# Opening of a backbone step: ten repeated filter products, the root taken ahead of the sine, and the second angle moved between two multiplications of x

## What is computed

```python
def rmsnorm(x, g):
    xf = x.astype(jnp.float32)
    y = xf * lax.rsqrt(jnp.mean(xf * xf, axis=-1, keepdims=True) + EPS)
    return (y * g.astype(jnp.float32)).astype(x.dtype)
...
    h = jnp.sin(freq * (feats @ fw1.astype(f32) + fb1.astype(f32)))
    h = jnp.sin(freq * (h @ fw2.astype(f32) + fb2.astype(f32)))
    h = (h @ fw3.astype(f32)).reshape(L, 2, 2, D_HY)
...
    sh1, sc1, g1, sh2, sc2, g2 = jnp.split(mod[:, None, :].astype(dt), 6, axis=-1)
    h = rmsnorm(x, n1) * (1 + sc1) + sh1
    u = h @ w_in
```

## Time and profile before

| | us |
|---|---|
| median of 3 runs | 2548.91 |
| lowest and highest run | 2544.83, 2552.96 |
| the profiled execution's own time | 2545.34 |
| its span in the profile | 2543.6 |

### The profile page before, as it was taken

The page is one execution under the profiler, slowest core; times in us unless marked ns, Lnnn a source line. Parts: engine busy times, 40 slices in busy tenths (PEclk is TensorE's granted clock), DMA queues, the critical chain, the costliest instruction groups (busy, mean ns, idle before and its releaser), DMA issues. The chain is left out here.

```text
span 2543.6 us, 34536 instructions
## 1 busy us (share of the span) xinstructions
PE 2466.6 (97%) x13482; PEld 2094.6 (82%) x13482; DVE 1420.8 (56%) x2694; ACT 613.9 (24%) x884; POOL 682.8 (27%) x300
## 2 busy tenths in 40 slices
PE   5999999999999999999899999999999999999997
PEld 3788888787878888888778878888888888888886
DVE  6887887687767666655753564633223332333226
ACT  5323233666563212212220012200000000000004
POOL 1222221222222222212134360343313422342320
PEclk9999999999999999999999999999999999999999
DMA  7344443211132232323372250111101110111002
GB/s 306 126 150 163 151 161 135 69 52 62 52 146 102 94 110 93 112 107 135 112 258 93 87 197 1 50 50 34 49 16 49 42 40 23 43 49 33 29 21 83
DMA packets 53835, 234.53 MB, mean 92 GB/s; under 512 B 6259, under 2 KB 8819, under 8 KB 48132
## 3 DMA queue, kind: packets, MB, share of 16 engines
q1 hardware_dynamic: 53764, 233.55, 25.5%
HBM read 179.00 MB, written 54.53 MB: 92 GB/s over the span
## 5 line engine op out<-in xcount | busy, mean ns | idle before, releaser
L851 PE MATMUL ps<-h_hi,w_hi 128*128 128x512 f32 (+1 forms) x2112 | 761.2, 360 | 15.8 <-DVE h_lo L1870 9.2
L852 PE MATMUL ps<-h_lo,w_hi 128*128 128x512 f32 (+1 forms) x2112 | 750.3, 355 | 0.0
L853 PE MATMUL ps<-h_hi,w_lo 128*128 128x512 f32 (+1 forms) x2112 | 750.2, 355 | 0.0
L809 POOL TENSOR_TENSOR w_hi<-w_raw,zero_col 128x1024 fp32r<-128x1024 f32 x96 | 203.1, 2116 | 1570.7 <-PE ps L853 1294.3
L851 PEld LDWEIGHTS ps<-h_hi,w_hi 128*128 128x128 f32 x2112 | 400.8, 190 | 81.3 <-issue 17.6
L853 PEld LDWEIGHTS ps<-h_hi,w_lo 128*128 128x128 f32 x2112 | 400.9, 190 | 56.9
L852 PEld LDWEIGHTS ps<-h_lo,w_hi 128*128 128x128 f32 x2112 | 401.1, 190 | 55.6 <-issue 0.2
L2231 DVE TENSOR_TENSOR a<-sil,ps 128x512 f32<-128x512 f32 (+1 forms) x66 | 39.5, 599 | 504.1 <-PE ps L853 501.8
L812 POOL TENSOR_TENSOR w_lo<-w_raw,w_hi 128x1024 fp32r<-128x1024 f32 x96 | 260.5, 2713 | 7.5
L2254 DVE SCALAR_TENSOR_TENSOR x<-ps,mod,x 128x512 f32<-128x512 f32 (+1 forms) x264 | 172.3, 661 | 98.1 <-PE ps L853 97.5
L852 PE MATMUL ps<-h_lo,wf_hi 128*128 128x512 f32 (+1 forms) x624 | 224.4, 360 | 0.0
(11 more groups left out here) (279 smaller groups left out, 3441.5 us busy)
## 6 DMA issues: line engine op xcount, KB each, us to landing
w_raw<-in_weights SPq DMA_DIRECT2D x146, 512.0 KB, 3.8
ada_w<-in_w_ada SPq DMA_DIRECT2D x18, 1024.0 KB, 7.9
scratch_gate_s<-g_st SPq DMA_DIRECT2D x24, 640.0 KB, 3.3
side<-scratch_gate_s SPq DMA_DIRECT2D x24, 640.0 KB, 3.9
scratch_k_s<-kstage SPq DMA_DIRECT2D x8, 1536.0 KB, 6.7
hy_k<-scratch_k_s SPq DMA_DIRECT2D x8, 1536.0 KB, 8.8
scratch_hy_s<-hout SPq DMA_DIRECT2D x16, 640.0 KB, 3.1
ada_early<-in_w_ada SPq DMA_DIRECT2D x6, 1024.0 KB, 22.1
```

What stands on the lines that cost most here:

```text
L809: nc.gpsimd.tensor_tensor(hi[:], w_raw[slot % 2][:], zero_col[:].to_broadcast([P, D]), ALU.add).then_inc(pool_step, 1)
L851: mm(out, w_pair[0], x_pair[0], start=first, stop=False)
L852: mm(out, w_pair[0], x_pair[1], start=False, stop=False)
L853: return mm(out, w_pair[1], x_pair[0], start=False, stop=last)
```

## The change

PE repeats one product of the first filter layer ten times behind that layer; the results go to the projection bank `ps[0]`, which nobody reads before it is written again, and no semaphore is signalled. PE computes the first row of the modulation ahead of the second filter layer instead of behind it. ACT takes the root ahead of the first sine, and takes the first row of the modulation out of PSUM ahead of the second filter layer. DVE reduces the second angle between the multiplication of the first 512 tokens and that of the second 512, instead of ahead of both. What is computed stays the same.

```diff
 FIRST_MIX = 3
+IDLE_PRODUCTS = 10
 MIX_BANKS = 5
...
             filter_layer(0, lambda rows: f_w1[:, :], lambda half, rows, a, e: feats[:, half * HALF_T + a:half * HALF_T + e])
 
+            for _ in range(IDLE_PRODUCTS):
+                mm(ps[0][0:FILT_HID, 0:512], f_w1[:, :], feats[:, 0:512], start=True, stop=True)
+
             pe.wait_ge(consts_set, 3)
             out, done = mix_unit(u_setup, 0, SQUARES_UNIT)
             pe.wait_ge(x_sq_summed, KD - 1)
...
             ins.then_inc(done, 1)
 
+            pe.wait_ge(csilu_set, 2)
+            row_product(0)
+
             pe.wait_ge(filt_in, 32)
             pe.wait_ge(sin_ready, 1)
             filter_layer(1, lambda rows: f_w2[rows, :], lambda half, rows, a, e: h1f[rows, a:e])
-
-            pe.wait_ge(csilu_set, 2)
-            row_product(0)
 
             pe.wait_ge(diag_ready, 1)
...
-            act.wait_ge(arg_ready, 1)
-            fn(h1f[:, :], arg[:, :], ACT.Sin).then_inc(sin_ready, 1)
             act.wait_ge(consts_set, 3)
             src, free = take_mix(u_setup, 0, SQUARES_UNIT)
             own(fn(rstd_col[:, :], src[:, 0:2 * NT], ACT.Sqrt, bias=eps[:, 0:1], scale=1.0 / D))
             act.sem_inc(free, 1)
             act.sem_inc(rms_ready, 1)
+            act.wait_ge(arg_ready, 1)
+            fn(h1f[:, :], arg[:, :], ACT.Sin).then_inc(sin_ready, 1)
+            take_row(0)
             take_filter(1)
-            take_row(0)
...
-            reduce_angle(1)
             for p in range(2):
+                if p:
+                    reduce_angle(1)
                 a, e, _ = PIECES[p]
```

## The result

| | before | changed |
|---|---|---|
| median of 7 runs, us | 2548.91 | 2559.26 |
| lowest and highest, us | 2544.83, 2554.22 | 2557.89, 2564.18 |
| ratio, 95% interval | 1 | 1.0047 (1.0037 to 1.0056) |
| profiled execution's own time, us | 2545.34 | 2557.89 |
| its span, us | 2543.6 | 2556.1 |

The changed kernel is slower by 0.47%, with an interval that leaves no change out. The ratio is not the quotient of the two medians, which is 1.0041 (10.4 us). The forecast was 2553.0 us and no measurable change; the time lies 0.2 us under the upper end of its range, and the kernel is slower, to which 0.17 had been given. What came is nearly the second rival.

A forecast was written before the change was run, and what follows sets the result against it. The prediction took DVE's chain to bound the opening. Root exchange and products gained 0; the new orders made the first product 4.1 us later: 2548.9 + 4.1 = 2553.0 us, range 2546.5 to 2559.5.

The forecast's parts named there:

- the second rival: PE: clock never rises in the ten products, sums end at 32.4 us or later; +10 us, slower; chance 0.12.
- What bounds the kernel: Opening: DVE's chain from root to `h_lo` sets the first projection product at 52.49 us; its shift is kept to the end.
- The root does not come earlier: ACT: the root's table load waits for the sums of the squares, so putting it ahead of the sine gains 0.
- What the ten products do: PE: ten products end about 22 us, sums stay at the lower clock; gain 0 (0 to 1.9 us).
- My reading of the hole: PE idle about 3 us before the sums: the clock falls almost at once, 0.4 us after the last work at 45.81.
- The order of ACT and PE: First sine ends at 33.25 instead of 29.31 us, second filter layer takes 1.4 us, first piece there at 35.85 us.
- The order of DVE: Second angle meets POOL's splits while `norm_a` and `u_t` run free; first product at 56.6 us, 4.1 us later (+1.0 to +6.6).
- The first: Rival on PE's clock: the products keep it up, sums end at 27.4 us; change 0; chance 0.16 for lasting or partly lasting.
- The third: Rival behind the opening: stretches at the lower clock move by some 2 us, widening every case, deciding none; no own chance.

The follow-up runs named there:

- experiment 12: Kernel before plus fourteen idle DVE multiplications behind the sixteen of x, nothing reordered; 2556.61 us, ratio 1.0035.
- experiment 1: Changed kernel with none of the ten repeated products, all reorderings kept; 2552.68 us, ratio 1.0018 to before.
- experiment 3: Changed kernel, its ten products over 128 rows and 128 columns instead of 17 and 64; 2552.86 us, ratio 1.0022 to before.
- experiment 5: Changed kernel, its ten products with 128 rows instead of 17, still 64 columns; executed once, 2547.76 us.
- experiment 6: Changed kernel, its ten products with 128 columns instead of 64, still 17 rows; executed once, 2555.59 us.
- experiment 9: Changed kernel with twelve full-array products, second filter layer behind the spreading products, second weight split after all of h, DFT constants awaited behind the first tile; 2547.76 us, 0.9994.
- experiment 7: Changed kernel without the ten products, POOL's weight splits held until the second angle is reduced; 2550.56 us, ratio 1.0008 to before.
- experiment 4: Changed kernel with the second angle put back ahead of all multiplications of x, products and other orders kept; 2557.22 us, ratio 1.0026 to before.
- second split late (8): Kernel before with POOL's second weight split after all of h and PE's wait for DFT constants behind the first projection tile; 2547.45 us, ratio 0.9996.
- experiment 10: Same as experiment 9 but without the twelve products; 2548.21 us, ratio 1.0000 to before.

## Why the prediction was wrong

**What bounds the kernel: held.** DVE's chain sets the first product, and its lateness goes through to the end (experiment 12).

**The root does not come earlier: held.** In experiment 1 the table load starts 0.1 us behind the sums, as before.

**What the ten products do: this step failed.** I wrote that ten products take between 9.7 and 19 us and took "the lower end plus a share at the low level", about 22 us for their end. They took 17.27 us and ended at 28.5. The ground for my choice was that the first projection tile had got its clock within 4 us of work; but that tile uses 128 rows, and the products 17. The row that should have weighed more was in view: the first filter layer, the same product, showed no rise. Experiments 3, 5 and 6 settle it. My reading of the hole, that the clock falls as soon as PE stops, was wrong as well (it outlasted 1.9 to 2.3 us in experiments 3, 5 and 9), but had no part in the result, since the clock never rose. The Trainium skill ("TensorE: Matmul & The Clock Gate", Part 1) says that "activity releases the throttle"; in these runs 17 us of gapless products with 17 rows did not, so for such products the measurement decides against a reading of it as any activity. The late sums are worth 3.0 us of the first product (9.2 against 6.2 with the starts taken off) and 0.29% of the time. The forecast of the first product, +4.1, missed 9.2 by 5.1 us: 3.0 are this step, the other 2.1 are the two sizes named below.

**The order of ACT and PE: mechanism held, one size off.** Sine behind a table load of 1.28 us, with no drain behind it (35.97 to 35.99); DVE idle for 3.06 us, forecast 2.9. The second filter layer was put at 1.4 us and took 2.38 where no products stand ahead (experiment 1) and 1.51 in the changed kernel.

**The order of DVE: mechanism held, size off.** The splits stretch the angle, shown both ways by experiments 1 and 7. I had two waits; there were three, since the angle came later by the terms above. `mod` waited 0.44 us for PE's last turns, which I had hidden with 1.6 us to spare: they ran at the lower clock, 3.58 us for 16 records against 1.96.

**The rivals.** The second, clock never rises, is what happened: +10 at the first product forecast, +9.54 measured. It had 0.12 and deserved more than the forecast. The first is what experiment 3 made of the kernel, at the first product. The third, that the stretches at the lower clock move, was taken to decide nothing; in the traced execution of experiment 9 such stretches take away the whole gain of the opening (below).

**What stays open.** The profiled executions differ by 12.6 us, the first products by 9.5. The kernel before was profiled in an execution 3.6 us under its median; the medians differ by 10.4 us, close to the 9.5. Where lateness grows or shrinks behind the opening can be read by laying the traces side by side. The table gives how much later than in the kernel before DVE starts the same instruction, each trace counted from its own first filter product. The first columns are the first projection product, `tsum` (87.17 us before), `hout` (98.85 us before) and the instruction that starts at 1251.3 us before. It is one profiled execution of each kernel; that of experiment 9 is 3.2 us above its kernel's median, so its last number says too much.

| us later than before | first product | `tsum` | `hout` | at 1251 | end |
|---|---|---|---|---|---|
| changed | 9.2 | 9.8 | 9.8 | 10.6 | 12.1 |
| no products (1) | 6.2 | 6.8 | 6.6 | 7.0 | 8.6 |
| full-array products (3) | 0.2 | 0.3 | 2.2 | 2.8 | 4.4 |
| angle back (4) | 3.2 | 3.5 | 7.2 | 8.7 | 13.4 |
| second split late (8) | -3.1 | -2.5 | -2.7 | -1.9 | -0.4 |
| all together, with products (9) | -3.4 | -2.8 | -0.5 | 2.9 | 5.1 |
| all together, without (10) | -1.8 | -1.5 | 1.8 | 3.0 | 5.5 |
| idle multiplications (12) | 7.3 | 7.1 | 6.8 | 7.0 | 9.0 |

In the changed kernel and in experiments 1 and 12 the lateness of the first product stays as it is for over 1,200 us. Experiments 3 and 9 lose 2 us between `tsum` and `hout`, where the clock stays at 0.50 for 13.7 us (from 74.7 and from 72.3 us) instead of 10.2 us before. Experiments 4 and 10 lose 3.7 and 3.3 us at the same place by another cause, the one of the opening over again. Two short instructions of DVE in the chain that makes `f_a` meet the next splits of POOL, and PE waits for that chain (3.7 us in experiment 10, 4.2 us in experiment 4), as it never does there in the kernel before:

```profile
95.47 1.92 POOL L810 TENSOR_TENSOR w_hi<-w_raw,zero_col 128x1024 fp32r<-128x1024 f32 x1 [8.99 <-PE ps L855]
95.56 1.98 DVE L224 TENSOR_TENSOR f_a<-f_t 128x128 f32<-128x128 f32 x1
97.47 2.47 POOL L813 TENSOR_TENSOR w_lo<-w_raw,w_hi 128x1024 fp32r<-128x1024 f32 x1
97.67 2.42 DVE L224 TENSOR_TENSOR f_a<-f_t 128x128 f32<-128x128 f32 x1
100.87 5.35 PE L971 MATMUL ps<-f_a,fwd 128*128 128x128 f32 x31 [3.70 <-DVEq L1982]
```

The same instruction takes 0.28 us where no split runs. Whether this wait is also what parts the two groups of runs of experiment 4 is not shown, as only one of its executions was traced. Further on, experiment 9 has two stretches of 6.8 us at 0.50 (from 451.2 and 802.8 us) where the kernel before has two of 3.4 us, and all eight kernels of the table have one more of 3.4 us between 1279 and 1295 us, in the changed kernel from 1291.8 us, that the kernel before lacks (so does experiment 7). Between 1251 us and the end the changed kernel loses 1.5 us, of the 2.9 us that its profile has beyond its first product. Windows with fixed bounds mislead here: from 1260 to 1320 us the clock is 0.91 in the changed kernel and 0.99 before, but the stretch of 6.8 us at 0.50 that both have starts at 1251.1 us before, ahead of that window, and at 1261.0 us, inside it, in the changed kernel. Why the clock differs at such places from kernel to kernel was not settled.

## What to carry to other kernels

Products put on an idle TensorE need not raise its clock: here those with 17 rows stayed at the lower level for 17 us. Read the spacing of their records before counting on their length, and make them end ahead of the operand that the next real product waits for. Before moving VectorE work, look at what GpSimd runs at the new place: VectorE instructions with SBUF operands alone waited until the running GpSimd instruction ended (`norm_a`, `u_t`, the angle, and `f_a` far behind the opening), those with a PSUM operand did not (0.61 us beside the splits and without them). An instruction moved into an idle slot of its engine is only free if the slot stays where it was; here sums that ended 3.5 us late cost 3.0 us more at the first product, on top of the 6.2 us of the new order.

## What the runs showed of the hardware

- Twenty f32 records of 512 columns: 17.27 us with 17 rows and 64 columns, 17.43 with 17 rows and 128 columns, 11.77 with 128 rows and 64 columns, 11.55 with 128 rows and 128 columns. Under the last two the clock rose after some 6 us.
- With the clock up, it outlasted 1.9 to 2.3 us without PE work (experiments 3, 5 and 9); ten sums with 2 columns then took 2.36 to 2.72 us instead of 4.40. In experiment 3 the clock was at 0.50 behind them, from 27.0 to 30.2 us, with PE busy all the time.
- VectorE and GpSimd alternate instruction by instruction when both want SBUF operands: a tensor_scalar of 0.56 us took 2.61 and a GpSimd split of 2.36 us took 2.93, each having waited for the other.
- A table load on ScalarE takes 1.28 us, and the ACTIVATE behind it starts 0.01 to 0.02 us later.
